# Positions added during mixing, two expert loads moved forward, and buffers cleared by another engine in a trunk layer on one Trainium2 core

## Chip, cores and metric

One core of one Trainium2 chip runs the whole program as one launch. The metric is the device time in microseconds. All arithmetic is 32-bit float, with a few integer steps in the routing. The names: PE is TensorE, PEld its weight load, DVE VectorE, ACT ScalarE, POOL GpSimd, SP SyncE, which issues most transfers.

## What is computed

One layer of a trunk over 128 prompt tokens and 512 sample tokens of width 1024. A bidirectional RWKV-7 scan and a gated convolution are mixed, projected by `w_out` and added to the tokens; then a mixture of experts (32 experts in 4 groups, two of one group for each token) is added, and a final norm follows. Cut to what matters here:

```python
xs = x_sample + grid_pos_embed(rows)          # positions: a constant table
def trunk_layer(x, cond, s0, p):
    sh1, sc1, g1, sh2, sc2, g2 = adaln_mod(cond, p['ada_w'], p['ada_b'])
    h = rms_norm(x, p['norm1_g']) * (1 + sc1) + sh1
    z = h @ p['w_in']
    y_rwkv, s_new = rwkv7_bidir(...)
    y_conv = conformer_conv(...)
    x = x + g1 * (concatenate([y_rwkv, y_conv]) @ p['w_out'])
    h = rms_norm(x, p['norm2_g']) * (1 + sc2) + sh2
    x = x + g2 * hier_moe(h, p)
    return x, s_new
```

## The kernel before

Each engine runs one program; they meet in semaphores. The stages follow one another in all of them: front (norm and modulation), mix, out, route, experts, overflow, end.

**Mix.** The columns of `w_in` are multiplied tile by tile ("z" steps, L582, a quarter tile each) while the scan's preparation and its steps are laced in between, in an order written out by hand for PE, ACT, DVE and SP (`ORDER`, L655). There are five scan units; four hold the sample tokens, the fifth the prompt. Each unit's preparation runs on DVE and ACT (L1050 to L1111: scans, scaled keys and their products) and feeds gram matrices on PE (L1275). GpSimd has nothing to do in this stage after it has stored the last block of modulation rows at L536. The convolution is done tile by tile in two buffers, `uin` and `cacc`; each of four tiles is stored to DRAM (L801) and loaded back at L858 when the scan's room is free. The last convolution tile is stored at about 205 us; the memory of `uin` and `cacc` (from `conv_at`) is unused from then on. The experts' weight buffers, six of 3 MB (`ebuf`, L1404), lie on top of the scan's memory; the first two lie over the buffers of the units with odd numbers.

**Out.** `sp_out` (L1467) loads the tokens again as residual rows `x2` (five tiles of 128 rows and 512 KB), the modulation rows `g1b`, `gain2`, `sh2b`, and stores the final states. PE multiplies tile after tile (order `WTILES`: 1, 2, 3, 4, 0) by `w_out`, two halves of 512 columns each (L1640, sixteen matmuls for a half), turns each finished tile (L1609) and computes its 36 router logits (L1624). `act_out` loads the positions of the next tile into one buffer `sq_pos` (L1892). On DVE, `residual` adds the positions (L1765) and then the gated projection in two halves (L1770, L1771); `taken` copies half of a turned tile out of a bank (L1757); `top_two` (L1793 to L1811) picks group and experts; `expert_input` (L1778 to L1784) forms the experts' input row, which ACT stores to DRAM with the residual rows (L1909, L1910). DVE's first wait in this loop is for all five residual tiles and both `g1b` rows (L1750).

**Route.** DVE and PE count rows per expert, sort the experts and write a table of slots (L1984 to L2062). The list of experts is ready at L2005 (`s_ids`), the table at L2060 (`s_tab`). GpSimd clears the row buffers `xe` with one memset when `w_out` is done (L2098), since tiles of a pair or of four can have empty rows.

**Experts.** 16 tiles of rows run in a fixed order: each needs one, two or four experts. GpSimd gathers each tile's rows (L2108) and scatters its results (L2114). PE turns the rows (L2332), multiplies by gate and up weights (L2348), turns the hidden rows (L2357) and multiplies by the down weights (L2369). SP loads 32 experts, 1 MB each for gate, up and down (L1510). The experts of the first three loads are fixed; they are loaded behind `sp_out`. The later ones need `s_ids`. The fourth load is issued at once, the fifth and sixth wait for the first gather (`s_gat[0]`), and from the seventh on each waits until the tile that used its buffer has been multiplied.

## Time and profile before

| | us |
|---|---|
| median of 3 runs (lowest, highest) | 1085.02 (1084.62, 1087.08) |
| the profiled execution | 1084.78 |
| its span | 1083.1 |
| PE busy | 899.6 (83%) |
| DVE busy | 590.1 (54%) |
| ACT busy | 287.6 (27%) |
| POOL busy | 61.7 (6%) |

The page also cuts the span in 40 slices of 27 us. These are its rows of busy tenths (9 is 90% or more), of TensorE's granted clock in tenths of full speed, and of the transfers:

```profile
PE   3899988999988697878967997796698797997786
DVE  5239999765267767677761455567524132331325
PEclk9899988999988677585685899797599898998998
DMA  9952642210100202001018168411599999999874
GB/s 355 329 217 59 238 187 100 82 59 10 21 2 11 22 1 31 3 11 21 2 21 195 51 210 346 178 59 78 189 421 420 420 420 406 406 422 382 337 272 197
```

Slice 24 begins at 623 us. The mix ends about there, out and route run to 776 us, the experts to about 1055 us. A busy engine is not by itself the bound of a stretch; the chain of waits and the idle time ahead of an instruction, with what ended it, tell that.

### The profile page before, as it was taken

The numbers are of one execution on the slowest core, as the hardware profiler recorded it, in microseconds if no ns is written. First come the engines' busy times: TensorE is split into PE (matmuls) and PEld (weight loads), VectorE is DVE, ScalarE is ACT, GpSimd is POOL, SyncE is SP. The second block draws the span as 40 slices with busy tenths as digits, with TensorE's granted clock in tenths as the row PEclk, the third lists the DMA queues.
The fourth block names the chain that finished last, engine by engine and source line by source line (L and its number), as shares of the span: only waits on it lengthen the run. The fifth ranks groups of instructions, "written<-read, shape, count | busy, mean of one in ns | idle before, by whom it ended". The sixth has DMA issues, their size and how long they took to land.

```text
span 1083.1 us, 17415 instructions
## 1 busy us (share of the span) xinstructions
PE 899.6 (83%) x6856; PEld 543.4 (50%) x6856; DVE 590.1 (54%) x1197; ACT 287.6 (27%) x506; POOL 61.7 (6%) x63
## 2 busy tenths in 40 slices
PE   3899988999988697878967997796698797997786
PEld 2466444567665675757747653444333242442232
DVE  5239999765267767677761455567524132331325
ACT  4230010331755646377212351011110000000002
POOL 0100000000000000000000000001111110111023
PEclk9899988999988677585685899797599898998998
DMA  9952642210100202001018168411599999999874
GB/s 355 329 217 59 238 187 100 82 59 10 21 2 11 22 1 31 3 11 21 2 21 195 51 210 346 178 59 78 189 421 420 420 420 406 406 422 382 337 272 197
DMA packets 74292, 194.74 MB, mean 180 GB/s; under 512 B 41888, under 2 KB 44354, under 8 KB 60004
## 3 DMA queue, kind: packets, MB, share of 16 engines
q1 hardware_dynamic: 65988, 175.30, 43.9%
q0 software_dynamic: 5728, 10.79, 2.7%
q10 hardware_dynamic: 2495, 7.54, 1.8%
q8 instruction: 55, 0.90, 0.3%
q14 instruction: 26, 0.21, 0.1%
HBM read 180.68 MB, written 21.31 MB: 187 GB/s over the span
## 4 chain that ended last, share of the span: by engine, by line
PE 44%; DVE 16%; DMA 13%; ACT 7%; issue 4%; SPq 1%; ACTq 0%; DVEq 0%
PE bank L2348 9%; PE bank L582 8%; DMA arena<-in_expert_w_up 8%; PE bank L2369 3%; DMA arena<-table_positions 3%; PE bank L1640 3%; DVE arena L1022 2%; PE bank L1262 2%; PE bank L1275 2%; PE bank L1332 2%; PE bank L1361 1%; ACT arena L898 1%; PE bank L1335 1%; DMA arena<-winv 1%; DVE arena L1119 1%
## 5 line engine op out<-in xcount | busy, mean ns | idle before, releaser
L582 PE MATMUL bank<-arena 128*128 128x320 f32 x704 | 207.3, 448 | 2.6 <-ACT arena L410 2.6
L582 PEld LDWEIGHTS bank<-arena 128*128 128x128 f32 x704 | 133.5, 194 | 77.0 <-issue 27.4
L2348 PE MATMUL bank<-arena 128*64 128x512 f32 (+2 forms) x496 | 124.0, 673 | 24.5 <-DMA arena<-in_expert_w_up 23.6
L1022 DVE SCALAR_TENSOR_TENSOR arena<-arena 128x655 f32<-128x655 f32 x116 | 104.7, 902 | 4.4
L2348 PEld LDWEIGHTS bank<-arena 128*64 128x64 f32 (+2 forms) x496 | 44.5, 152 | 102.3 <-issue 101.0
L2451 DVE TENSOR_TENSOR arena<-arena,bank 128x256 f32<-128x256 f32 x16 | 6.7, 422 | 130.9 <-ACT arena L2410 130.9
L1640 PE MATMUL bank<-arena 128*128 128x512 f32 x160 | 74.5, 622 | 0.0
L2369 PE MATMUL bank<-arena 128*64 128x512 f32 (+2 forms) x248 | 58.8, 599 | 9.4 <-DVE arena L2454 9.4
L2410 ACT ACTIVATE arena<-bank 128x256 f32<-128x256 f32 x16 | 6.2, 385 | 201.9 <-PE bank L2348 201.8
L1640 PEld LDWEIGHTS bank<-arena 128*128 128x128 f32 x160 | 31.0, 198 | 37.3 <-issue 37.1
L1361 PE MATMUL bank<-arena 64*64 64x64 f32 x320 | 33.1, 263 | 13.0 <-DVE arena L1189 13.0
L1361 PEld LDWEIGHTS bank<-arena 64*64 64x64 f32 x320 | 27.8, 170 | 25.8 <-DVE arena L1189 19.2
L2369 PEld LDWEIGHTS bank<-arena 128*64 128x64 f32 (+2 forms) x248 | 19.2, 138 | 38.1 <-issue 25.7
L1119 DVE TENSOR_TENSOR arena<-bank,arena 128x512 f32<-128x512 f32 x40 | 27.7, 693 | 14.9 <-PE bank L1275 13.9
L2098 POOL MEMSET arena<- 128x4096 f32 x1 | 3.5, 3512 | 541.1 <-PE bank L1640 541.1
L981 ACT ACTIVATE arena<-bank 64x128 f32<-64x128 f32 (+1 forms) x68 | 19.9, 292 | 51.9 <-PE bank L1361 45.6
L1050 DVE SCALAR_TENSOR_TENSOR arena<-arena 128x512 f32<-128x512 f32 (+1 forms) x48 | 26.6, 553 | 12.8 <-ACT arena L898 11.2
L1189 DVE TENSOR_TENSOR arena<-bank,arena 64x128 f32<-64x128 f32 (+1 forms) x68 | 20.9, 307 | 21.4 <-PE bank L1352 18.7
L1275 PE MATMUL bank<-arena 64*128 64x128 f32 x320 | 25.9, 305 | 7.2 <-issue 1.7
L898 ACT ACTIVATE arena<-arena 128x512 f32<-128x512 f32 (+1 forms) x48 | 27.0, 563 | 15.1 <-DVE arena L1134 6.3
L1262 PE MATMUL bank<-arena 128*128 128x512 f32 x40 | 28.2, 804 | 2.3 <-ACT arena L917 2.3
L1297 PE MATMUL bank<-arena 64*64 64x64 f32 x320 | 28.4, 255 | 1.7 <-ACT arena L908 1.7
(360 smaller groups left out, 1351.2 us busy)
## 6 DMA issues: line engine op xcount, KB each, us to landing
arena<-in_expert_w_gate SPq DMA_DIRECT2D x33, 1024.0 KB, 18.7
arena<-in_expert_w_up SPq DMA_DIRECT2D x33, 1024.0 KB, 24.3
arena<-in_expert_w_down SPq DMA_DIRECT2D x33, 1024.0 KB, 23.5
arena<-in_ada_w SPq DMA_DIRECT2D x12, 2048.0 KB, 10.4
arena<-in_w_in SPq DMA_DIRECT2D x22, 512.0 KB, 4.4
arena<-expert_rows SPq DMA_DIRECT2D x10, 512.0 KB, 7.3
arena<-in_x_sample SPq DMA_DIRECT2D x8, 512.0 KB, 6.8
arena<-in_w_out SPq DMA_DIRECT2D x1, 4096.0 KB, 15.3
```

What stands on the lines that cost most here:

```text
L582: mm = nc.tensor.matmul(psum[4 + 2 * (n % 2) + half][:, 0:HALF], wring[:, n % NWIN, k], hT[:, k, half * HALF:(half + 1) * HALF], start=(pa ...
L898: ins_ = nc.scalar.activation(X[:, s[4]:s[4] + s[3]], previous(zrkv[:, 4 * m + s[1], :], s), ACT.Copy, scale=par[:, c:c + 1])
L1022: chain(nc.vector.scalar_tensor_tensor(acc, src, w, acc, ALU.mult, ALU.add))
L1050: ins_ = nc.vector.scalar_tensor_tensor(x, current(zrkv[:, 4 * m + s[1], :], s), oneminus[:, c:c + 1], x, ALU.mult, ALU.add)
L1119: chain.announce(nc.vector.tensor_tensor(GM[b][:, GC * (q % 2) + 4 * (q // 2):GC * (q % 2) + 4 * (q // 2) + 4, :], psum[BANK[f"g{q}"]][:, ...
L1262: nc.tensor.matmul(psum[BANK[f"{name}{h}"]][:, :], headones, T0[:, 512 * h:512 * h + 512], start=True, stop=True).then_inc(s_summed, 1)
L1275: mm = nc.tensor.matmul(psum[BANK[f"g{q + h}"]][:, n * P:(n + 1) * P], BK[r, gc_, :], AR[b][r, gc_, :], start=True, stop=True)
L1297: mm = nc.tensor.matmul(psum[BANK[f"m{q}"]][0:64, n * C:(n + 1) * C], GM[b][64:128, GC * h + g0 + n, 0:C], SAV[b][64:128, g0 + n, C * h:C ...
L1361: mm = nc.tensor.matmul(psum[6 + h][0:64, k * C:(k + 1) * C], GM[b][0:64, GC * h + gc_, 0:C], XS[0:64, at:at + C], start=True, stop=True)
L1640: mm = nc.tensor.matmul(psum[2 * ((q + 1) % 2) + n][:, :], lhs, wout[:, c, n * 512:(n + 1) * 512], start=(c == 0), stop=(c == 7))
L2348: mm = nc.tensor.matmul(psum[2 + n % 2][r, :], xeT[:, n % 2, c, r], gu[:, :, c, :], start=(c == 0), stop=(c == KD - 1))
L2369: mm = nc.tensor.matmul(psum[5 + h][r, :], hidT[:, n % 2, c, r], wd[:, c, h * 512:(h + 1) * 512], start=(c == 0), stop=(c == 1))
```

## The change

Four things are done.

1. `pool_mix`, new: when the convolution's tiles are stored, GpSimd loads each of the four sample tiles and its positions into the free memory at `conv_at`, adds them, and stores the sum to `placed` in DRAM. `sp_out` takes the residual rows of tiles 1 to 4 from there. The adds in `residual`, the buffer `sq_pos`, its loads on ACT and the semaphore `s_pos2` go. The load of tile 4 counts in `s_modb`, so that DVE's first wait is for six loads.
2. `sp_out` begins with the loads of the first two fixed experts, behind waits for `placed` and for the last step of the fourth unit. The third follows behind `sp_out`. After the lists two experts are loaded ahead of the wait for the first gather, not one.
3. The buffers `xe` are cleared by four ACT copies with scale 0 (`act_route`), which now runs inside `act_out`, ahead of the last tile's stores. `pool_experts` waits for it.
4. For the last tile, the row's scale is computed on its own (`row_scale`), then `top_two`, then `expert_input`.

```diff
+        placed = dram("tokens_with_positions", [TS, D])
+        tok_in, pos_in = view(conv_at, D), view(conv_at + D, D)
+        def pool_mix(chain):
+            pool = nc.gpsimd
+            for stored in s_cst:
+                pool.wait_ge(stored, 32)
+            for i in range(1, TILES):
+                if i > 1:
+                    pool.wait_ge(s_placest, 16 * (i - 1))
+                pool.dma_start(tok_in, tok_src(i)).then_inc(s_sl, 16)
+                pool.dma_start(pos_in, pos[(i - 1) * P:i * P, :]).then_inc(s_sl, 16)
+                pool.wait_ge(s_sl, 16 * 8 + 32 * i)
+                chain(nc.gpsimd.tensor_tensor(tok_in, tok_in, pos_in, ALU.add))
+                pool.dma_start(placed[(i - 1) * P:i * P, :], tok_in).then_inc(s_placest, 16)
 ...
         def sp_out():
             sp = nc.sync
+            sp.wait_ge(s_placest, 16 * (TILES - 1))
+            sp.wait_ge(s_Y, step_at(NU - 2, steps(NU - 2) - 1) + 1)
+            for n in range(len(FIXED_EXPERTS) - 1):
+                experts_load(n)
             sp.wait_ge(s_gvar, 5)
-            for i in (1, 2, 3, 0):
-                sp.dma_start(x2[:, i], tok_src(i)).then_inc(s_x2in, 16)
+            for i in (1, 2, 3):
+                sp.dma_start(x2[:, i], placed[(i - 1) * P:i * P, :]).then_inc(s_x2in, 16)
+            sp.dma_start(x2[:, 0], tok_src(0)).then_inc(s_x2in, 16)
 ...
-            sp.dma_start(x2[:, 4], tok_src(4)).then_inc(s_x2in, 16)
+            sp.dma_start(x2[:, 4], placed[3 * P:4 * P, :]).then_inc(s_modb, 16)
 ...
-            dve.wait_ge(s_x2in, 16 * (TILES + 2))
+            dve.wait_ge(s_x2in, 16 * (TILES + 1))
 ...
             def residual(q, n):
-                if i and n == 0:
-                    dve.wait_ge(s_pos2, 16 * i)
-                    chain(nc.vector.tensor_tensor(x2[:, i], x2[:, i], sq_pos, ALU.add))
 ...
-            dve.wait_ge(s_modb, 16 * 6)
+            dve.wait_ge(s_modb, 16 * 7)
 ...
             residual(q, 1)
             taken(q)
+            row_scale(q)
+            top_two(q)
             expert_input(q)
-            top_two(q)
 ...
             for q, i in enumerate(WTILES):
-                if i:
-                    if q:
-                        act.wait_ge(s_x2, 2 * (q - 1) + 1)
-                    act.dma_start(sq_pos, pos[(i - 1) * P:i * P, :]).then_inc(s_pos2, 16)
 ...
+                if q == TILES - 1:
+                    act_route(chain)
                 act.wait_ge(s_h2, q + 1)
 ...
         def act_route(chain):
             act = nc.scalar
+            act.wait_ge(s_wo, 2 * TILES)
+            for n in range(NG):
+                ins_ = nc.scalar.activation(xe[:, n], ones[:, 0:1].broadcast_to([P, D]), ACT.Copy, scale=0.0)
+                if n < NG - 1:
+                    chain(ins_)
+            chain.announce(ins_, s_ge, 1)
             act.wait_ge(s_mx, TILES)
 ...
-        def pool_route(chain):
-            pool = nc.gpsimd
-            pool.wait_ge(s_wo, 2 * TILES)
-            chain(nc.gpsimd.memset(xe, 0.0))
 ...
         def pool_experts(chain):
             pool = nc.gpsimd
+            pool.wait_ge(s_ge, 1)
             pool.wait_ge(s_tab, 1)
 ...
             sp_out()
-            sp.wait_ge(s_pos2, 16)
-            for n in range(len(FIXED_EXPERTS)):
-                experts_load(n)
+            experts_load(len(FIXED_EXPERTS) - 1)
             sp.wait_ge(s_ids, 1)
             sp.wait_ge(s_h2st, 32 * TILES)
             sp.dma_start(gain_step[0:2], modrows[:, 5 * D:6 * D]).then_inc(s_fg, 16)
-            experts_load(len(FIXED_EXPERTS))
+            for n in range(len(FIXED_EXPERTS), NB - 1):
+                experts_load(n)
             sp.wait_ge(s_gat[0], 16)
-            for n in range(len(FIXED_EXPERTS) + 1, NB):
-                experts_load(n)
+            experts_load(NB - 1)
```

## Rows read from the trace of the kernel before

**Rows 1.** Timeline of PE, 640 to 760: start, us, line, shapes, [idle before, releaser].

```profile
648.26 14.00 PE L1640 MATMUL bank<-arena 128*128 128x512 f32 x32
...
669.53 1.04 PE L1609 MATMUL bank<-arena 128*128 128x128 f32 x8
683.84 3.63 PE L1624 MATMUL bank<-arena 128*128 128x36 f32 x16 [13.28 <-DVE arena L1832]
...
703.26 1.04 PE L1609 MATMUL bank<-arena 128*128 128x128 f32 x8
704.54 1.98 PE L1624 MATMUL bank<-arena 128*128 128x36 f32 x16 [0.25 <-ACT arena L1885]
...
720.17 1.04 PE L1609 MATMUL bank<-arena 128*128 128x128 f32 x8
...
733.38 1.03 PE L1609 MATMUL bank<-arena 128*128 128x128 f32 x8
```

**Rows 2.** The chain of waits from 640 on: start, us, what.

```profile
665.55 15.20 DMA arena<-table_positions
```

**Rows 3.** Busy us by engine in two stretches; last the clock, DMA share, GB/s.

```profile
205.00:255.00 50.00, 48.29 (x224) 32.56 (x223) 28.01 (x36) 18.27 (x28) 0.00 (x0) 1.00 0.16 50
...
780.30:843.00 62.70, 52.27 (x214) 21.32 (x213) 19.64 (x31) 5.83 (x11) 9.91 (x10) 0.94 1.01 410
```

**Rows 4.** Timeline of PE in the expert stage.

```profile
779.60 1.97 PE L2332 MATMUL bank<-arena 128*128 128x128 f32 x8 [0.60 <-DMA arena<-tokens_for_experts,arena]
...
843.09 9.81 PE L2348 MATMUL bank<-arena 128*32 128x512 f32 x64 [5.47 <-DMA arena<-in_expert_w_up]
```

**Rows 5.** Timeline of DVE, 649 to 1061.

```profile
649.63 0.09 DVE L1813 MEMSET arena<- 128x32 f32 x1 [9.14 <-DMA arena<-in_x_sample]
...
743.11 3.57 DVE L1807 TENSOR_SCALAR arena<-arena 128x32 f32<-128x32 f32 x1
...
748.09 0.69 DVE L1771 TENSOR_TENSOR arena<-arena 128x512 f32<-128x512 f32 x1
...
752.78 1.28 DVE L1784 SCALAR_TENSOR_TENSOR arena<-arena 128x1024 f32<-128x1024 f32 x1
754.10 0.25 DVE L1793 SCALAR_TENSOR_TENSOR arena<-bank,arena 128x36 f32<-128x36 f32 x1
...
758.48 0.21 DVE L1984 TENSOR_SCALAR arena<-arena 2x128 f32<-2x128 f32 x1
...
1060.90 0.69 DVE L2511 TENSOR_TENSOR arena<-arena,bank 128x512 f32<-128x512 f32 x1 [3.92 <-issue]
```

**Rows 6.** Timeline of GpSimd (POOL).

```profile
743.13 3.51 POOL L2098 MEMSET arena<- 128x4096 f32 x1 [541.11 <-PE bank L1640]
776.07 1.09 POOL L2108 DMA_INDIRECT arena<-tokens_for_experts,arena  x1 [29.42 <-DVE arena L2060]
...
1060.99 2.37 POOL L2189 TENSOR_TENSOR arena<-arena 128x1024 f32<-128x1024 f32 x1 [0.22 <-DMA arena<-expert_rows]
```

**Rows 7.** Timeline of ACT: a 128x1024 activation.

```profile
748.87 1.06 ACT L1904 ACTIVATE arena<-arena 128x1024 f32<-128x1024 f32 x1 [4.68 <-DVE arena L1771]
```

**Rows 8.** Timeline of SP's queue: issue time, us of issuing.

```profile
204.58 0.33 SPq L801 DMA_DIRECT2D conv_out<-arena  x1
...
780.31 0.34 SPq L1510 DMA_DIRECT2D arena<-in_expert_w_gate  x1
```

**Rows 9.** DMA issues: count, KB each, median us from issue to landing.

```profile
residual_rows<-arena ACTq DMA_DIRECT2D x5, 512.0 KB, 3.9
...
arena<-tokens_for_experts,arena POOLq DMA_INDIRECT x18, 10.9
```

**Rows 10.** Timelines of DVE and PE in the mixing.

```profile
229.36 1.13 DVE L1082 TENSOR_SCALAR arena<-arena 128x512 f32<-128x512 f32 x2
...
240.41 1.54 DVE L1111 SCALAR_TENSOR_TENSOR arena<-arena 128x512 f32<-128x512 f32 x2
...
240.48 1.16 PE L1275 MATMUL bank<-arena 64*128 64x128 f32 x16 [1.71 <-issue]
```

More of the change, by code:

```diff
@@ L784, in build @@
         s_cst = [sem(f"conv_tile_stored{b}") for b in range(2)]
+        s_placest = sem("placed_tokens_stored")
         def sp_mix():
@@ L1427, in build @@
         g1b, gain2 = regs.take(2, D), regs.take(2, D)
-        h2, sq_pos = regs.take(D), regs.take(D)
+        h2 = regs.take(D)
         rwg, lgc = regs.take(2, KD * 36), regs.take(2, 36)
@@ L1450, in build @@
         s_cn, s_mixc = sem("conv_normed"), sem("conv_mixed")
[L1451 removed]
+        s_x2in = sem("residual_landed")
         s_wo, s_x2, s_h2, s_h2st = (sem(n) for n in (
@@ L1771, in residual, with row_scale @@
                 chain.announce(nc.vector.tensor_tensor(x2[:, i, o], x2[:, i, o], xtmp[:, o], ALU.add), s_x2, 2 * q + n + 1)
+            def row_scale(q):
+                i = WTILES[q]
+                dve.wait_ge(s_xstat, TILES + q + 1)
+                chain.announce(nc.vector.tensor_scalar(small[:, i:i + 1], small[:, i:i + 1], 1.0 / D, RMS_EPS,
+                                                     ALU.mult, ALU.add), s_var, TILES + q + 1)
+                dve.wait_ge(s_std, TILES + q + 1)
+                chain(nc.vector.reciprocal(small[:, 16 + i:17 + i], small[:, 8 + i:9 + i]))
             def expert_input(q):
@@ L1778, in expert_input @@
                 chain(nc.vector.tensor_tensor(h2, x2[:, i], gain2[:, int(i > 0)], ALU.mult))
-                dve.wait_ge(s_xstat, TILES + q + 1)
-                chain.announce(nc.vector.tensor_scalar(small[:, i:i + 1], small[:, i:i + 1], 1.0 / D, RMS_EPS,
-                                                     ALU.mult, ALU.add), s_var, TILES + q + 1)
-                dve.wait_ge(s_std, TILES + q + 1)
-                chain(nc.vector.reciprocal(small[:, 16 + i:17 + i], small[:, 8 + i:9 + i]))
+                if q < TILES - 1:
+                    row_scale(q)
                 chain.announce(nc.vector.scalar_tensor_tensor(h2, h2, small[:, 16 + i:17 + i], sh2b[:, int(i > 0)],
@@ L1844, in dve_out @@
             taken(q)
+            row_scale(q)
+            top_two(q)
             expert_input(q)
-            top_two(q)
         def act_out(chain):
@@ L2065, in act_route @@
             act = nc.scalar
+            act.wait_ge(s_wo, 2 * TILES)
[4 more added lines that the diff above has]
+            chain.announce(ins_, s_ge, 1)
             act.wait_ge(s_mx, TILES)
-            chain.announce(nc.scalar.activation(gexp, gexp, ACT.Exp), s_ge, 1)
-            chain.announce(nc.scalar.activation(t3, t3, ACT.Exp), s_ge, 2)
+            chain.announce(nc.scalar.activation(gexp, gexp, ACT.Exp), s_ge, 2)
+            chain.announce(nc.scalar.activation(t3, t3, ACT.Exp), s_ge, 3)
         def pe_route():
@@ L2561, in _ @@
             act_out(chain)
-            act_route(chain)
             act_table()
@@ L2582, in _ @@
             pool_front()
-            pool_route(chain)
+            pool_mix(chain)
             pool_experts(chain)
```

8 lines of the change are left out of this document (4 added, 4 removed).

## Prediction

> **What bounds the kernel now.** I read the 40 slices of the page first (PE at 9 tenths almost everywhere, DMA at 9 only from slice 29 on), then the chain of waits after the mixing, then the timelines of PE, DVE, GpSimd and SyncE's queue over the stretches that the chain names. Times are positions in the profiled span. Three stretches matter. From 205 to 285 us PE is full, and the change puts new GpSimd work beside it. From 640 to 776 us (output projection and routing) PE stops: it stands for 13.28 us ahead of the logits of the first tile [rows 1], because DVE waits for a 512 KB tile of positions, which took 15.20 us to land [rows 2] while the nine loads of three fixed experts filled the queues. From 780 us on the expert weights stream at 410 GB/s with the DMA share at 1.01 [rows 3]; PE waits for them at the four-expert tiles (5.47 us at 843.09 [rows 4]). So an earlier start helps in full only if the stream starts earlier too.
>
> **Position waits (a gain).** In the changed kernel the residual rows come with positions in them, so four adds on DVE and four loads on ScalarE's queue go. DVE's first wait now lasts until 649.63 and ends with an in_x_sample tile [rows 5], the one for tile 4, which the change counts in another semaphore; the six loads that are left in that wait should be in by about 645. Even a start at 649.6 would be free: DVE's next residual needs the second half of tile 1, which is the first half of PE's 14.00 us block from 648.26 and ends at 655.3 [rows 1]. DVE then has its residuals, gains, first expert input and prompt mixing done by about 668.7 (I follow the same instructions as now without the positions). PE's turn of the first tile stays at 669.53 [rows 1], and its logits follow at once. From there PE bounds the loop. An undisturbed round, turn to turn, is 720.17 - 703.26 = 16.91 us [rows 1] (this one had a late position tile too, but it held up DVE, not PE). DVE has about 11 us of work in a round: top-two 758.48 - 754.10 = 4.4 [rows 5], residuals and copy some 3.6, expert input 3.3. So the second turn comes at 669.53 + 16.91 = 686.4 in place of 703.26: **16.8 us**. The third keeps this. Between third and fourth turn lies one half less, 16.91 - 7.0 = 9.9 us, where the trace has 733.38 - 720.17 = 13.2 [rows 1] (DVE's copy late by a position tile, and a slower matmul block): **3.3 us** more.
>
> **Row buffers cleared by ScalarE (a gain).** GpSimd's memset ran from 743.13 for 3.51 us [rows 6], and DVE's TENSOR_SCALAR at 743.11 took as long, 3.57 us, where a TENSOR_SCALAR of 2x128 takes 0.21 [rows 5]; it stood in the top-two that holds back the last residual. Without it **3.3 us** go. The four ScalarE copies cost about 1.06 us each, as the 128x1024 Square does [rows 7]: 4.3 us, between the last root and the exponentials. DVE's top-two (4.4 us) covers them, so nothing is on the path; without that cover it would be at most 4.3. Together the last residual, now done at 748.09 + 0.69 = 748.8 [rows 5], comes 23.4 us sooner, at 725.4.
>
> **New order behind it (a loss).** Top-two no longer waits for the last expert input, but for the logits: about 1 us behind the residual for the turn, then sixteen matmuls, 3.63 us with PE cold (683.84) and 1.98 warm (704.54 [rows 1]), so 3.0 to 4.6 us behind it. Then come 4.4 us of top-two and 2.6 us of expert input (two 128x1024 instructions, 1.28 the longer [rows 5]). Route starts 10.0 to 11.6 us behind the residual; now it is 758.48 - 748.8 = 9.7. Cost 0.3 to 1.9; PE idles less than before, so near the low end: **-0.7**. Left: 22.7 us at the table of slots.
>
> **Two fixed experts earlier, one more between lists and gather.** The two early loads (6.3 MB, 15.4 us at 410 GB/s) are issued at about 597 us, behind the convolution's loads on the same queue, into a stretch that is empty until 632. Nothing else is queued behind them but the waits on SyncE, which come later. The third still goes out near 656. After the lists, SyncE now issues two experts ahead of its wait for the first gather, not one: now one near 763, then nothing until 780.31 [rows 8]. In the changed kernel the lists are ready near 740, but the last store of rows (it is behind the moved expert input, and such a store takes 3.9 us to land [rows 9]) makes it about 742. Two experts, 6.3 MB, then run until 742 + 1.7 + 15.4 = 759. The gather is issued at 776.07 - 22.7 = 753.4 [rows 6], and would land 3.5 us later on an empty fabric; beside the loads its median is 10.9 us [rows 9], so it crawls until 759 and lands at about 760. PE starts to turn the rows at 779.60 [rows 4]; then at 760: 19.6 us sooner. Cost of the contention **-3.1** (0 if it shares evenly, 7.4 if it takes the median).
> What a page would make of this: the Trainium skill, "DMA: Bandwidth & Descriptors", section "Queues, rings and completion order", says that each engine goes round between the queues it has work for, packet by packet. Read as even shares that would let the gather land near 758.5 and give 1.5 us back (1061.5); the median of 10.9 us under load speaks against it, so the sum goes by the row.
>
> **The stream.** Counted from the first gather, the stream has one expert less to bring: 3.15 MB, 7.7 us. Against it stands new idle time, since six buffers are then full until the first gate-up matmuls end (9.4 us after they start): 2 to 3 us. PE's wait of 5.47 us at the first four-expert tile [rows 4] thus shrinks to a rest below 1: **+4.6** (bounds 0 and 5.5). From there on the stream is full, and everything, tail included, keeps its distances.
>
> **GpSimd in the mixing (a loss).** Twelve DMAs and four 128x1024 adds of 2.37 us [rows 6] begin once the last convolution tile, stored at 204.58 [rows 8], has landed. A turn of that loop is two loads (some 4 us), the add, and a store (some 3 us) that the next turn waits for, about 11 us: adds near 212, 223, 234 and 245, over by 251, far ahead of 632. DVE works without a pause from 229.36 or earlier to 240.41 + 1.54 = 241.95, and PE already waits 1.71 us for this at 240.48 [rows 10]. The add near 234 falls into it. The trace has two cases of GpSimd beside DVE: the memset that stopped a TENSOR_SCALAR with both ends in the arena, and an add at 1060.99 beside which L2511, with one operand in a bank, took 0.69, as L1771 does [rows 5, 6]. DVE's instructions here have all operands in the arena, and two of them are TENSOR_SCALARs of that form [rows 10]. I take the blocked case for one add: **-2.35**; bounds 0 and 4.7 (two adds). The others meet DVE where it has slack, or reads a bank. PE is full from there to 285, so nothing gives it back.
> The page "SBUF — State Buffer" of the Trainium skill (its practical consequences of port sharing) says that a DVE instruction with two SBUF inputs and a GpSimd instruction that reads SBUF shut each other out, and that a DVE one with one SBUF input outside the 2-port modes is free. No row here shows the two-input case. If only the TENSOR_SCALAR form blocked, the sum would lose this term most likely (1060.6).
>
> **Sum.** 16.8 + 3.3 + 3.3 - 0.7 - 3.1 + 4.6 - 2.35 = 21.85 us. The profiled execution took 1084.78 us (span 1083.1), the median of the runs is 1085.02, 0.2 above. 1085.0 - 21.9 gives **1063.1**.
>
> **Rivals.**
> - No add holds up DVE's chain: 1060.7. For it, L2511; against it, L1807. 0.22.
> - The gather takes its median of 10.9 us, so PE starts 4.3 us later than I have it, and the four-expert tile waits as now (4.6): 1067.4 to 1072. For it, the median of 18 gathers; against it, that only the second half of two loads runs beside it. 0.18.
> - The change does less than it says: the position wait was a wait for the shared queues, and the one fixed expert still issued near 656 (7.7 us) holds up the stores of the first tile, for which DVE's second expert input waits. Then 1070.8. Against it, that stores of DVE's first input leave at 665, when that load is through. 0.07.
> - Slower than before: DVE gets nothing done while GpSimd runs its 44 us loop. DVE is busy for 28.0 us between 205 and 255 [rows 3]; put behind the loop, they cost 28.0 - 2.35 us more than in the sum, 1088.8. It decides from 24 us of blocked DVE on. The adds last 9.5 us in all, so 0.02.
> - My forecast, with the terms within their near bounds (1061.3 to 1066): 0.51.
>
> **How the numbers follow.** Likeliest 1063.1. To hold 8 in 10 the range takes in the first rival with a fully saved quad wait and even sharing (1058) and the second up to 1069. What a measurement can tell from no change is about 0.2%, 2.2 us. Faster needs under 1082.9, which all but the last rival give: 0.975; same 0.01; slower 0.015.
>
> **What the profile would show.** PE's wait at the first logits gone and its second turn near 689 (686.4 plus the 2.35 of the mixing); no 3.5 us DVE instruction near the last top-two; DVE's last residual near 728; first gather landed near 762; less than 1 us of wait at the first four-expert tile; an add of GpSimd inside DVE's chain near 234, with one DVE instruction 2 us too long, and PE's wait at 240 grown to 4. I am wrong if the gather lands over 5 us behind the end of the loads, if PE waits for DVE inside the rounds, or if z quarters start late by more than one add.

## The result

The changed kernel takes **1070.66 us** (median of 4 runs, 1068.16 to 1072.89) where the kernel before takes 1085.74 beside it (4 runs). The ratio is 0.9858, 95% interval 0.9838 to 0.9878: 1.4% faster. Three runs that lie far above all others of their kernels (1456.11 us in e1, 1108.04 in e2, and 3813.41 of the kernel before in the group of e5, e6, e7 and a2) are left out of the medians and ratios.

The direction of the forecast holds. Its time, 1063.1, is 7.6 us too low, and the range of 1058 to 1069 does not hold the result. Later groups gave the same changed kernel ratios of 0.9862 (0.9824 to 0.99) and 0.9875 (0.9849 to 0.9902).

The profiled execution of after took 1072.89 us (span 1071.2, against 1083.1 before). From the page:

| | before | after |
|---|---|---|
| span, profiled | 1083.1 us | 1071.2 us |
| PE busy | 899.6 us (83%) | 905.6 us (85%) |
| GpSimd (POOL) busy | 61.7 us (6%) | 74.0 us (7%) |
| GpSimd's DMA queue | 10.79 MB | 17.09 MB |

The page's slices of after, GpSimd and the granted clock in tenths (one slice is 26.8 us):

```profile
POOL 0100000131000000000000000000101111011023
PEclk9899988998987759585586699997599899999899
```

Slices 8 to 10 (counted from 1, 187 to 268 us) hold what is new: GpSimd works in them, and in the tenth the clock reads 8 where it is 9 in before.

First what the forecast said of the output stage. PE's timeline in after, the turns of the five token tiles (the rows that answer to [rows 1]):

```profile
679.20 1.04 PE L1632 MATMUL bank<-arena 128*128 128x128 f32 x8
680.58 1.95 PE L1647 MATMUL bank<-arena 128*128 128x36 f32 x16 [0.34 <-ACT arena L1912]
...
696.17 1.04 PE L1632 MATMUL bank<-arena 128*128 128x128 f32 x8
...
713.09 1.04 PE L1632 MATMUL bank<-arena 128*128 128x128 f32 x8
...
723.20 1.04 PE L1632 MATMUL bank<-arena 128*128 128x128 f32 x8
...
735.33 0.66 PE L1632 MATMUL bank<-arena 128*128 128x128 f32 x4 [2.01 <-DVE arena L1791]
```

The logits wait 0.34 us where they waited 13.28, the second turn comes 16.97 us behind the first (forecast 16.91), the fourth 10.11 behind the third (9.9), and the second half of the last one 12.1 behind that. Only the first turn stands in the wrong place: 679.20, 9.7 us later than in before [rows 1]. All of that was lost ahead of the output stage, in the mixing: 8.4 us of it up to 260 us, 2.2 from there to 649 us, where the traces scatter by more than that (below), less 0.9 us by which after was ahead at 199 us. VectorE and PE in before, where the first addition will fall and at one of the instructions that the third will meet:

```profile
212.08 1.54 DVE L1050 SCALAR_TENSOR_TENSOR arena<-arena 128x512 f32<-128x512 f32 x2 [1.75 <-ACT arena L898]
215.25 1.12 PE L1262 MATMUL bank<-arena 128*128 128x512 f32 x2
...
232.31 1.23 DVE L1087 TENSOR_TENSOR arena<-arena 128x1024 f32<-128x1024 f32 x1
```

VectorE, GpSimd and PE in after (L1068 is the L1050 of before, L1105 its L1087, L1280 its L1262):

```profile
211.25 3.51 DVE L1068 SCALAR_TENSOR_TENSOR arena<-arena 128x512 f32<-128x512 f32 x2 [1.75 <-ACT arena L916]
211.83 2.38 POOL L875 TENSOR_TENSOR arena<-arena 128x1024 f32<-128x1024 f32 x1 [4.10 <-DMA arena<-table_positions]
...
216.39 1.16 PE L1280 MATMUL bank<-arena 128*128 128x512 f32 x1 [1.93 <-ACT arena L935]
...
235.07 2.35 POOL L875 TENSOR_TENSOR arena<-arena 128x1024 f32<-128x1024 f32 x1 [4.48 <-DMA arena<-table_positions]
235.16 3.35 DVE L1105 TENSOR_TENSOR arena<-arena 128x1024 f32<-128x1024 f32 x1
...
245.44 2.08 PE L1293 MATMUL bank<-arena 64*128 64x128 f32 x16 [3.84 <-issue]
...
247.59 0.69 DVE L1137 TENSOR_TENSOR arena<-bank,arena 128x512 f32<-128x512 f32 x1
247.66 2.35 POOL L875 TENSOR_TENSOR arena<-arena 128x1024 f32<-128x1024 f32 x1 [5.65 <-DMA arena<-table_positions]
```

Two additions, not one, have a VectorE instruction beside them that is about 2 us too long (3.51 for 1.54, 3.35 for 1.23), and PE waits behind each: 1.93 us at 216, where before has no wait, and 3.84 where [rows 10] has 1.71. Behind the second wait sixteen matmuls of L1293 take 2.08 us where [rows 10] has 1.16. The fourth addition runs beside L1137, which reads a bank, and costs it nothing. Busy time by engine, clock, DMA share and GB/s in two stretches, first of before, then of after:

```profile
205.00:235.00 30.00, 30.00 (x109) 19.71 (x108) 14.77 (x19) 17.05 (x24) 0.00 (x0) 1.00 0.22 64
235.00:260.00 25.00, 23.29 (x136) 16.32 (x136) 13.24 (x18) 2.41 (x6) 0.00 (x0) 1.00 0.13 32
```

```profile
205.00:235.00 30.00, 28.07 (x96) 17.94 (x95) 14.01 (x16) 14.62 (x21) 9.16 (x10) 0.94 0.53 185
235.00:260.00 25.00, 21.16 (x116) 14.80 (x115) 16.71 (x19) 2.06 (x4) 6.92 (x6) 0.86 0.33 119
```

The granted clock, 1.00 in before, is 0.94 and 0.86. Two short stretches right behind the waits show where it was down, at the lower of its two levels (1.2 and 2.4 GHz):

```profile
216.40:219.50 3.10, 3.10 (x5) 1.68 (x6) 0.69 (x1) 0.00 (x0) 1.07 (x2) 0.51 0.42 110
245.40:247.40 2.00, 1.96 (x16) 1.81 (x16) 1.93 (x3) 0.00 (x0) 0.00 (x0) 0.50 0.73 299
```

The clearing of the row buffers and the expert stage of after (rows that answer to [rows 7], [rows 6] and [rows 4]):

```profile
737.29 4.32 ACT L2093 ACTIVATE arena<-arena 128x1024 f32<-128x1024 f32 x4
742.43 1.28 ACT L2098 ACT_TABLE_LOAD   x1 [0.82 <-DVE arena L1837]
```

```profile
763.12 1.07 POOL L2134 DMA_INDIRECT arena<-tokens_for_experts,arena  x1 [512.23 <-DVE arena L2085]
```

```profile
769.93 1.97 PE L2359 MATMUL bank<-arena 128*128 128x128 f32 x8 [1.31 <-DMA arena<-tokens_for_experts,arena]
...
827.72 7.07 PE L2375 MATMUL bank<-arena 128*32 128x512 f32 x64 [0.75 <-DMA arena<-in_expert_w_up]
845.43 10.01 PE L2375 MATMUL bank<-arena 128*64 128x512 f32 x32 [4.83 <-DMA arena<-in_expert_w_up]
```

The wait of the first four-expert tile is gone (0.75 for 5.47 [rows 4]), but the next tile now waits 4.83. In before it waits 1.77:

```profile
860.49 7.09 PE L2348 MATMUL bank<-arena 128*64 128x512 f32 x32 [1.77 <-DMA arena<-in_expert_w_up]
```

**One execution is not the kernel.** Seventeen traces were taken in all, four of them of the kernel before. The time between fixed VectorE instructions splits each into stages. The marks, in after's lines, are the L1042 that starts at 198.65 in after (ahead of the first unit; in all traces it starts between 197.6 and 200.7), the last row of L1137 in that unit (259.50), L1743 (649.02, start of the output stage), L1780 (724.33), L2009 (744.97, start of the routing), L2448 (772.04, first expert tile) and the L2478 at 835.40 (first four-expert tile) and at 1003.25 (last static tile), and L2310 (1023.39, first overflow tile). Stage lengths in us, worked out from VectorE's timelines:

```
                      to 259 to 649 to 724 to 745 to 772 to 835 to 1003 to 1023
before                 52.48 387.28  95.16  23.97  23.22  71.81  165.03  16.74
b2_before_again        52.53 389.75  93.88  23.82  25.69  68.25  164.23  20.14
b3_before_again        52.30 389.35  94.07  23.83  25.69  68.38  163.77  20.13
b4_before_again        52.36 387.31  95.13  23.98  25.70  66.41  165.20  18.48
e3_loop_alone          58.15 385.01  93.47  23.84  25.69  68.98  163.97  16.75
after                  60.85 389.52  75.31  20.64  27.07  63.36  167.85  20.14
a2_after_again         58.30 386.29  75.30  20.78  27.23  64.56  166.11  16.76
a3_after_again         56.86 391.66  75.30  21.49  27.47  63.70  167.72  19.77
e7_double_add          60.71 388.45  75.30  21.59  27.03  63.83  167.73  19.68
e4_one_ahead           58.19 385.34  75.31  20.65  25.69  66.29  167.25  16.74
e5_memset_back         58.15 387.53  75.30  25.77  27.09  64.68  166.22  19.62
e6_fixed_late          58.27 388.70  75.30  20.65  27.13  63.47  167.82  19.71
e1_no_add              52.51 389.61  75.29  21.50  27.12  64.32  166.96  20.16
e11_memset_not_add     52.74 389.72  75.30  21.49  27.11  64.19  168.25  16.75
e10_copy_not_add       54.16 387.32  75.30  20.74  27.00  66.18  165.60  18.47
e2_gated               52.41 387.18  75.29  22.35  27.58  63.99  166.29  16.75
e8_gated_again         52.47 389.56  75.30  21.49  27.18  64.69  166.67  20.17
```

Behind the last mark all take 47.7 to 48.3. Read down a column: where all kernels with a part of the change differ from all without, it is the part; where one kernel differs from itself, it is the execution. "To 649" (385.0 to 391.7 over all) and "to 1023" are of the second kind.

### The profile page after: what moved, and what is told of

The parts are those of the page before. It is cut to its first block, busy times and chain, and to the rows that moved or that the text cites. A ratio compares the mean times of both kernels' runs of the same rounds, so it can differ in the third digit from the quotient of the medians.

```text
span 1071.2 us, 17424 instructions
## 1 busy us (share of the span) xinstructions
PE 905.6 (85%) x6856; PEld 547.9 (51%) x6856; DVE 585.8 (55%) x1193; ACT 291.9 (27%) x510; POOL 74.0 (7%) x78
## 3 DMA queue, kind: packets, MB, share of 16 engines
q0 software_dynamic: 7456, 17.09, 4.3%
## 4 chain that ended last, share of the span: by engine, by line
PE 49%; DVE 15%; DMA 10%; ACT 6%; issue 3%; SPq 1%; DVEq 0%; ACTq 0%; POOLq 0%
PE bank L2375 9%; PE bank L582 8%; DMA arena<-in_expert_w_up 7%; PE bank L1663 6%; PE bank L2396 4%; DVE arena L1040 2%; PE bank L1293 2%; PE bank L1353 2%; PE bank L1350 2%; PE bank L1280 1%; ACT arena L916 1%; PE bank L1379 1%; DMA arena<-winv 1%; PE bank L1305 1%; DVE arena L1137 1%
## 5 line engine op out<-in xcount | busy, mean ns | idle before, releaser
L582 PE MATMUL bank<-arena 128*128 128x320 f32 x704 | 212.1, 456 | 2.4 <-ACT arena L410 2.4
L2478 DVE TENSOR_TENSOR arena<-arena,bank 128x256 f32<-128x256 f32 x16 | 6.8, 422 | 124.9 <-ACT arena L2437 124.9
L1663 PE MATMUL bank<-arena 128*128 128x512 f32 x160 | 70.6, 595 | 0.0
L2134 POOL DMA_INDIRECT arena<-tokens_for_experts,arena x17 | 17.2, 1015 | 521.9 <-DVE arena L2085 512.2
L1379 PE MATMUL bank<-arena 64*64 64x64 f32 x320 | 32.3, 258 | 14.1 <-DVE arena L1207 14.0
L1137 DVE TENSOR_TENSOR arena<-bank,arena 128x512 f32<-128x512 f32 x40 | 27.7, 693 | 18.0 <-PE bank L1293 17.0
L1293 PE MATMUL bank<-arena 64*128 64x128 f32 x320 | 27.3, 317 | 9.7 <-issue 3.8
L1068 DVE SCALAR_TENSOR_TENSOR arena<-arena 128x512 f32<-128x512 f32 (+1 forms) x48 | 28.5, 594 | 12.0 <-ACT arena L916 10.5
L999 ACT ACTIVATE arena<-bank 64x128 f32<-64x128 f32 (+1 forms) x68 | 19.9, 292 | 52.0 <-PE bank L1379 50.5
L1280 PE MATMUL bank<-arena 128*128 128x512 f32 x40 | 28.7, 818 | 3.7 <-ACT arena L935 3.7
L1293 PEld LDWEIGHTS bank<-arena 64*128 64x128 f32 x320 | 23.4, 219 | 16.2 <-issue 15.6
L1305 PE MATMUL bank<-arena 128*128 128x128 f32 x160 | 28.2, 317 | 4.1 <-DVE arena L1085 1.7
```

Of the source, the lines that this page charges most:

```text
L582: mm = nc.tensor.matmul(psum[4 + 2 * (n % 2) + half][:, 0:HALF], wring[:, n % NWIN, k], hT[:, k, half * HALF:(half + 1) * HALF], start=(pa ...
L1068: ins_ = nc.vector.scalar_tensor_tensor(x, current(zrkv[:, 4 * m + s[1], :], s), oneminus[:, c:c + 1], x, ALU.mult, ALU.add)
L1137: chain.announce(nc.vector.tensor_tensor(GM[b][:, GC * (q % 2) + 4 * (q // 2):GC * (q % 2) + 4 * (q // 2) + 4, :], psum[BANK[f"g{q}"]][:, ...
L1280: nc.tensor.matmul(psum[BANK[f"{name}{h}"]][:, :], headones, T0[:, 512 * h:512 * h + 512], start=True, stop=True).then_inc(s_summed, 1)
L1293: mm = nc.tensor.matmul(psum[BANK[f"g{q + h}"]][:, n * P:(n + 1) * P], BK[r, gc_, :], AR[b][r, gc_, :], start=True, stop=True)
L1305: mm = nc.tensor.transpose(psum[BANK[f"{name}{q}"]][:, n * P:(n + 1) * P], src, ident)
```

## The experiments

**e1: no additions.**

```
-                chain(nc.gpsimd.tensor_tensor(tok_in, tok_in, pos_in, ALU.add))
```

> The kernel after without the four GpSimd additions of L875; its loads and stores stay, so the rows of the last four token tiles lack their positions. Theory (in the mixing stage VectorE's instructions with two inputs in SBUF wait behind a GpSimd addition, two of the four additions lie on PE's path, and the granted clock falls after each): out's first matmul L1663 comes about 9 us earlier relative to the start than in the kernel after, and the time is 1061 to 1063 us (1070.7 less 8 to 10), a ratio to the kernel before near 0.978. L1068 at about 210 us falls from 3.51 to 1.54 for two, L1105 at about 235 us from 3.35 to 1.23. Rival (the descriptors, the loads and stores of GpSimd, or a clock that drifts with the chip): the time stays at 1069 to 1072 us and the stalls stay.

Measured: a median of 1065.2 us (5 runs), a ratio of 0.9799 (0.977 to 0.9829). The first stage takes 52.51 us, as in before, though GpSimd's twelve transfers are all there. It is the additions and not the traffic. L1068 is back at 1.54 us and the two-input instructions near 235 us at 1.23. The 8 to 10 us expected, and with them 1061 to 1063 us, are missed: the gain is about 6 in the time (from the 1071.1 of all runs of the kernel after, below). The trace of after, from which they were worked out, is the dearest of its kind in the first column.

**e2: the same additions, in VectorE's calm.**

```
                 pool.wait_ge(s_sl, 16 * 8 + 32 * i)
+                if i == 1:
+                    pool.wait_ge(s_rk, 1)
+                elif i == 3:
+                    pool.wait_ge(s_inv, 1)
+                elif i == 4:
+                    pool.wait_ge(s_cs, 2)
                 chain(nc.gpsimd.tensor_tensor(tok_in, tok_in, pos_in, ALU.add))
```

> The kernel after with the same four additions, each held back to a stretch in which VectorE has no instruction with two inputs in SBUF: the first behind the bonus product of the first unit (about 242 us), the second follows it by some 11 us, the third behind the inverse of the first unit (about 271 us), the fourth behind the decay sums of the second unit (about 296 us). The output is whole. Theory (lock, then clock): no stall of VectorE, out's first matmul about 9 us earlier than in the kernel after, 1061 to 1064 us. Rival (any GpSimd addition costs, wherever it lies, through its traffic or its power): 1068 to 1072 us. If the stall alone were gone but the clock fell anyway: about 1066 us.

Measured: a median of 1066.1 us (5 runs), a ratio of 0.9816 (0.9789 to 0.9842). The first stage takes 52.41 us with all four additions in the kernel. GpSimd's and VectorE's rows at the first one:

```profile
242.50 2.35 POOL L881 TENSOR_TENSOR arena<-arena 128x1024 f32<-128x1024 f32 x1 [33.30 <-DVE arena L1135]
```

```profile
242.91 1.42 DVE L1143 TENSOR_TENSOR arena<-bank,arena 128x512 f32<-128x512 f32 x2
```

L1143 has one input in a bank and takes its 1.42 us. The third and fourth addition lie behind the first stage, at 272 and 296 us, in a column that is as in before. So the same four additions cost nothing in these places; the rival "any addition costs" falls. The time is 2 us above the 1061 to 1064 expected and equals the 1066 of the rival "the clock falls anyway", but the trace rules that one out: the granted clock is 1.00 from 205 to 300 us.

**e3: the loop alone, on the kernel before.**

```
             sp.wait_ge(s_pos2, 16)
+            sp.wait_ge(s_placest, 16 * (TILES - 1))
             for n in range(len(FIXED_EXPERTS)):
...
+            pool_mix(chain)
```

> The kernel before with GpSimd's loop of loads, additions and stores alone; nobody reads what it stores, and the residual adds its positions as before. Its price by itself. By the trace of the kernel after: two additions on the path and the clock after them, 8 to 10 us slower than the kernel before, 1093 to 1095 us. By the forecast's step (one addition on the path, 2.35 us): 1087.4 us. By the rival that the lost time of the mixing stage is a matter of the execution and not of the loop: within 1 us of 1085.

Measured: a median of 1089.9 us (12 runs), a ratio of 1.0039 (1.0021 to 1.0056), 4.2 us above the kernel before by the ratio: between the two theories (1093 to 1095, and 1087.4). Its first stage is 58.15, 5.7 longer than the 52.4 of the kernel before, and no other column is longer than in before. Two VectorE instructions are too long again, 3.71 us near 212 (for 1.54) and this one:

```profile
235.85 2.48 POOL L874 TENSOR_TENSOR arena<-arena 128x1024 f32<-128x1024 f32 x1 [4.28 <-DMA arena<-table_positions]
236.15 3.26 DVE L1112 SCALAR_TENSOR_TENSOR arena<-arena 128x1024 f32<-128x1024 f32 x1
```

**e7: every addition twice.**

```
                 chain(nc.gpsimd.tensor_tensor(tok_in, tok_in, pos_in, ALU.add))
+                chain(nc.gpsimd.tensor_tensor(pos_in, tok_in, pos_in, ALU.add))
```

> The kernel after with every GpSimd addition of the mixing stage followed by a second one of the same size, whose result nobody reads. Theory (VectorE's two-input instructions wait behind GpSimd's additions, and the clock falls with the stalls): each blocked instruction lasts up to 4.7 us and not 3.4, and more of them are hit, since GpSimd adds for 19 us of some 56 and not for 9.4 of 45: 4 to 10 us slower than the kernel after, 1075 to 1081 us. Rival (the additions themselves cost nothing, the loss of the mixing stage comes from elsewhere): within 1.5 us of 1070.7.

Measured: a median of 1070.5 us (6 runs), a ratio of 0.985 (0.9819 to 0.9881). By the time the expectation of 4 to 10 us more is a miss. The trace says what happened in its place. The doubled turn lasts 14 to 16 us and not 11, so the additions meet other instructions:

```profile
229.15 2.88 POOL L875 TENSOR_TENSOR arena<-arena 128x1024 f32<-128x1024 f32 x1 [4.99 <-DMA arena<-table_positions]
229.86 4.95 DVE L1101 TENSOR_SCALAR arena<-arena 128x512 f32<-128x512 f32 x2
...
243.47 3.26 DVE L1126 TENSOR_TENSOR arena<-arena 128x1024 f32<-128x1024 f32 x1
...
245.73 3.21 POOL L876 TENSOR_TENSOR arena<-arena 128x1024 f32<-128x1024 f32 x1
...
246.83 2.08 PE L1294 MATMUL bank<-arena 64*128 64x128 f32 x16 [7.58 <-issue]
```

More instructions are held up, as expected, but none for two additions: the two instructions of L1101 take 2.46 us each (for 0.57), one beside each addition (the second addition runs from 232.11 for 2.42 us). The first addition meets the scan L1077 (3.26 us for 1.23) and no longer L1069 (the L1068 of after), and PE has no wait at 216. Its second wait has grown to 7.58 us for the 1.71 of before, and behind it the matmuls lose 2.4 us. Together that is the first stage of 60.71, 2.5 us longer than the 58.2 of most single-addition traces and no longer than that of after. The times do not tell these 2.5 us.

**e10 and e11: a copy, and a memset, in the additions' place.**

```
-                chain(nc.gpsimd.tensor_tensor(tok_in, tok_in, pos_in, ALU.add))
+                chain(nc.gpsimd.tensor_copy(pos_in, tok_in))      e10
+                chain(nc.gpsimd.memset(pos_in, 0.0))              e11
```

> The kernel after with a GpSimd copy (one input in SBUF) where the addition (two inputs) stood; the rows of the last four tiles lack their positions. A look at what on GpSimd's side holds VectorE. If any GpSimd instruction that reads SBUF does, L1068 or its neighbours still last longer than 1.54 us by about the copy's own length, and so do those at 235 us; if only a two-input instruction of GpSimd does, they show 1.54 and 1.23 us and the mixing stage loses nothing.

> The kernel after with a GpSimd memset (no input, it only writes) of one row buffer where the addition stood; the rows of the last four tiles lack their positions. If VectorE waits for any GpSimd instruction that touches SBUF, L1068 and L1105 or their neighbours grow by about the memset's length; if it waits only for one that reads, they stay at 1.54 and 1.23 us. The last residual of the kernel before took 3.57 us beside a memset, so by that row a stall is expected.

One run each (1063.15 and 1063.56 us); the rows of the last four tiles go without their positions here, as in e1. Timelines of GpSimd and VectorE at the third turn, e10 first:

```profile
231.89 1.04 POOL L875 COPY arena<-arena 128x1024 f32<-128x1024 f32 x1 [4.27 <-DMA arena<-table_positions]
232.01 1.99 DVE L1105 TENSOR_TENSOR arena<-arena 128x1024 f32<-128x1024 f32 x1
```

```profile
231.21 0.95 POOL L875 MEMSET arena<- 128x1024 f32 x1 [4.24 <-DMA arena<-table_positions]
231.32 1.23 DVE L1105 TENSOR_TENSOR arena<-arena 128x1024 f32<-128x1024 f32 x1
```

Beside the copy L1105 lasts 0.76 us longer (and L1068, near 212, 2.20 us for 1.54); beside the memset it takes its 1.23, and L1068 its 1.54. The first stages are 54.16 and 52.74 us. So VectorE's instruction with two inputs in SBUF waits for a GpSimd instruction that reads SBUF, for what is left of it, and not for one that only writes. That is what the Trainium skill says in "SBUF — State Buffer", section "Who interferes with whom", and the rows agree on both sides.

**a2: the kernel after once more.**

> The kernel after, unchanged, once more, on the same chip as the other kernels of this group: 1068 to 1073 us by its four executions so far. Its trace tells what belongs to one execution and what to the kernel: theory has a loss of 6 to 10 us in the mixing stage in every execution (the stalls of L1068 or its neighbours and of L1105 or its neighbours are there in each), while the 3.4 us that the stretch behind 1000 us lost to the granted clock is a matter of the execution and may be gone.

Measured: a median of 1068.9 us (6 runs, 1063.10 to 1074.03). Its first stage is 58.30, its "to 1023" 16.76 for 20.14 in the first trace. The loss in the mixing comes back, though with 5.9 us just under the 6 to 10 expected; that in the last tiles does not.

**e5: the memset back on GpSimd.** The four ScalarE copies go, and before GpSimd's wait for the table stands again

```
+            pool.wait_ge(s_wo, 2 * TILES)
+            chain(nc.gpsimd.memset(xe, 0.0))
```

> The kernel after with the row buffers cleared by GpSimd again (the 3.5 us memset of before, behind the last product of the output stage) and not by ScalarE. The forecast's step: the last residual of VectorE waits 3.3 us for the memset, everything behind it is 3.3 us later: 1074 us (1070.7 plus 3.3), and the row of the last residual shows about 3.5 us for what takes 0.4 to 1.2 us in the kernel after. Rival (a slack behind it takes it up, as the routing waits for something else): the same 1070.7.

Measured: a median of 1073.5 us (6 runs), a ratio of 0.9896 (0.9859 to 0.9933), 2.5 above the 1071.1 that the three groups of the kernel after give together (16 runs). VectorE and GpSimd in e5:

```profile
729.53 3.56 DVE L1833 TENSOR_SCALAR arena<-arena 128x32 f32<-128x32 f32 x1
729.55 3.51 POOL L2141 MEMSET arena<- 128x4096 f32 x1 [477.41 <-PE bank L1663]
```

The 3.3 us stall is back to the tenth. The stage grows from 20.6 to 22.4 (all others with the change) to 25.77, that is by 3.4 to 5.1. The stall is the forecast's. And here a memset does hold up VectorE: a TENSOR_SCALAR with one input in SBUF. The Trainium skill names that form too, in "SBUF — State Buffer", section "Who interferes with whom" (an instruction of VectorE's 2-port modes and any of GpSimd's), and lets a two-input one pass beside a memset, as e11 shows.

**e6: the two fixed experts late again.** Their loads move from the head of the output stage's SyncE list to its end, in front of the third.

> The kernel after with the two early loads of fixed experts put back behind the output stage's loads, as in the kernel before; the order of the routed experts' loads stays new. By the forecast the early loads carry nothing by themselves, since the stretch of 640 to 750 us moves only some 180 GB/s: within 1 us of the kernel after, 1070 to 1072 us. Rival: the transfers of the output stage's rows and of the fourth unit compete with the 6.3 MB (at 400 GB/s some 16 us of all queues), so that the residual's rows or the first routed expert come late: 2 to 8 us slower, with a wait for DMA at the first residual or at the first expert tile.

Measured: a median of 1069.5 us (6 runs), a ratio of 0.9857 (0.9828 to 0.9885), and every stage from 649 us on as in after within 0.5 us (75.30, 20.65, 27.13, 63.47, 167.82, 19.71). The early loads carry nothing by themselves; the rival falls.

**e4: one routed expert ahead of the first gather.**

```
-            for n in range(len(FIXED_EXPERTS), NB - 1):
-                experts_load(n)
+            experts_load(len(FIXED_EXPERTS))
             sp.wait_ge(s_gat[0], 16)
-            experts_load(NB - 1)
+            for n in range(len(FIXED_EXPERTS) + 1, NB):
+                experts_load(n)
```

> The kernel after with one routed expert's load ahead of the wait for the first gather in SP's queue, as before, and not two. The two fixed experts stay early. By the forecast's steps: the first gather lands sooner by some 3.3 us (less traffic beside it), and the wait of the four-expert tile L2348/L2371 for its weights comes back by 4.6 to 5.1 us: 1.3 to 1.8 us slower than the kernel after, near 1072.3 us. If the next wait for weights (4.83 us at 845 us) swallows what that step gains, the time is the same or 1 to 2 us less than the kernel after.

Measured: a median of 1070.6 us (6 runs), a ratio of 0.9855 (0.9817 to 0.9892). The gather's stage is 25.69 for 27.07 (1.4 sooner, not 3.3), the next 66.29 for 63.36 (2.9 later, not 4.6 to 5.1): up to the first four-expert tile (745 to 835 us) the second expert ahead is worth 1.6 us in the trace, up to 1003 us 0.7 against the mean of the traces with it, which is within their scatter, and it is worth nothing that the times can tell. The other theory of that line, 1 to 2 us less than after, isn't shown either.

**b2, b3, b4: the kernel before, three more traces.** No edit.

> The kernel before, unchanged, for its trace alone. If the 3.0 to 3.4 us that 7 of 12 traces with the change lose between the last static tile and the overflow tile (L2396 5.35 us for 3.65, L2234 8.80 for 7.10) belong to the change, every trace of the kernel before shows 3.65 and 7.10; if they are a matter of the execution, some of three show the long ones.

> The kernel before a second time. As for b2_before_again; the distance from the last static tile's residual (1018.54) to the first of the overflow (1035.28) is 16.7 us in the trace of before so far, and 19.7 to 20.2 in the slow traces of the kernel after.

> The kernel before a third time. As for b2_before_again. It also tells how far the stretch from 300 to 640 us scatters in the kernel before; with the change it differed by up to 6 us from trace to trace.

PE's last static tile and first overflow tile in b2:

```profile
1018.19 5.35 PE L2369 MATMUL bank<-arena 128*64 128x512 f32 x16 [0.58 <-DVE arena L2454]
...
1027.50 8.80 PE L2207 MATMUL bank<-arena 128*128 128x512 f32 x16 [2.87 <-DVE arena L2281]
```

These are the long ones. The stage is 20.14 and 20.13 us in two of the three, 18.48 in the third, 16.74 in the trace on which the forecast rested. So the 3.4 us are a matter of the execution, with and without the change. The same three show something else: the gather's stage is 25.7, not 23.22, and the first four-expert tile waits about 3 us (2.42 to 3.10), not 5.47. That trace was unusual twice. The first shows in PE's row of the eight matmuls of one row ahead of the first expert tile, in before and then in b2:

```profile
774.36 4.64 PE L2379 MATMUL bank<-arena 2*128 2x512 f32 x8
```

```profile
774.92 7.19 PE L2379 MATMUL bank<-arena 2*128 2x512 f32 x8
```

The granted clock is 0.78 over the first of these rows and 0.50 over the second.

The stretch from 259 to 649 scatters by 2.5 us between the four traces of before and by 6.3 between the twelve with the change; nothing here says whether the change adds to it.

**a3 and e8: after and the gated version, side by side.**

> The kernel after, unchanged, beside e8_gated_again: 1069.8 us, by the median of its ten executions so far (1063.1 to 1074.0). In its trace the loss up to 260 us is 5.7 to 8.4 us; the last 70 us take either what they take in the kernel before or 3.4 us more.

> The kernel after with its four additions held back to VectorE's calm stretches (the version of e2_gated, unchanged), once more beside the kernel after on one chip. Theory: nothing is lost up to 260 us in any execution (the first kernel-after executions lost 5.7 to 8.4 us there), so it is 3 to 7 us faster than the kernel after in the same group, 1062 to 1068 us in the median; the spread of some 7 us between executions stays, since it comes from the granted clock behind 300 us. Rival (the advantage of e2_gated was a matter of the execution): no more than 1.5 us faster.

Measured: after 1073.4 us (6 runs), ratio 0.9875 (0.9849 to 0.9902); gated 1065.6 us (6 runs), ratio 0.9803 (0.9779 to 0.9827). The intervals are apart. The 7.8 us between the medians are a little over the 3 to 7 expected, and after is 3.6 above the 1069.8 expected. First stages: 56.86 and 52.47. The loss of 4.4 us in a3 is below the 5.7 to 8.4 expected, and its trace says why: the first addition came too late to hold L1068 (1.55 us) and held the scan behind it, L1076 (3.27 us for 1.23), and PE had no wait there; only the second wait (3.68) was left. All runs taken together give 1071.1 (16) and 1066.1 (11), 5.0 us, near the 6.0 that the first stages show in the mean. **The gated version beats both kernels**: up to 260 us the positions cost nothing when GpSimd adds where VectorE reads a bank or waits.

## Why the forecast was half right

- **Position waits (16.8 and 3.3): right.** The turns stand at the distances forecast, in every trace with the change: that stage is 75.30 us, 19.9 shorter than in the trace of before, and 19.0 shorter than in the mean of the five traces that add the positions in the output stage (before four times, and e3). Forecast: 20.1.
- **Memset (3.3) and new order (-0.7): right in their sum.** Forecast together 2.6; 3.3 in the two profiles, 2.7 in the means. Only the memset was also taken back by itself (e5); no run shows the new order alone. The four copies of 4.32 us lie beside VectorE's top-two, and the exponentials behind them wait for VectorE, as [rows 7] and [rows 5] had it.
- **Gather (-3.1): right in size for the wrong baseline.** 3.85 between the two profiles, 1.4 against the 25.69 of the four other traces without the change. Without the second expert ahead it is nothing (e4). In those four the eight matmuls of one row (L2379 in before) run 7.19 us at the lower clock and not 4.64, and PE comes to its first tile later without any wait for rows; so part of the gather's time is hidden in most executions.
- **The stream (+4.6): the second step that failed.** The tile gained what was forecast (4.7), but "from there on the stream is full, and everything keeps its distances" is wrong: the very next tile waits 4.83 us where before has 1.77, and 3.1 go back. Against the four other traces without the change, whose means at these two tiles are 3.2 and 3.3 us, the first tile gained 2.3 us in the three traces of the changed kernel and the next gave back 1.6. I take the transfers of all weights together for the bound of both tiles (a DMA share of 1.01 in [rows 3]); no run changes how much is moved, so that is argued and not shown. From 745 to 1003 us the five traces without the change take 258.4 us in the mean, the ten with it (e4 and e5 left out) 258.5: the order of loads bought nothing.
- **GpSimd in the mixing (-2.35): the step that failed first and most.** The loss is 4.4 to 8.4 us in the seven traces with single ungated additions (6.0 in the mean, e3 included), 0 without the additions or with gated ones. What was priced came true: the addition near 234 makes one VectorE instruction about 2 us too long, and PE's wait at 240 grows to 3.84 (forecast 4). Two things were missed. The addition near 212 was taken for harmless ("the others meet DVE where it has slack"), though VectorE's instruction there feeds ScalarE and, through it, PE: some 2 us. And behind the waits PE's clock was down, which no term had. The row that the price leaned on, [rows 6], shows a TENSOR_SCALAR held up by a memset; which forms an addition holds up was open, and the runs show two-input ones (SCALAR_TENSOR_TENSOR, TENSOR_TENSOR, TENSOR_TENSOR_SCAN) as well as a TENSOR_SCALAR (e7). In e6, a trace of the usual kind:

```profile
216.78 1.12 PE L1280 MATMUL bank<-arena 128*128 128x512 f32 x2 [2.09 <-ACT arena L935]
...
244.05 2.08 PE L1293 MATMUL bank<-arena 64*128 64x128 f32 x16 [3.75 <-issue]
246.06 3.06 PE L582 MATMUL bank<-arena 128*128 128x320 f32 x8
```

The waits are 2.09 and 2.04 more than before (3.75 less the 1.71 of [rows 10]), and the slow matmuls 1.6 (2.08 for 1.16, 3.06 for 2.42): 5.7 us, the stage's 5.8. In the trace of after the clock fell behind the first wait too, and the slow matmuls are over 4 us. The term's bounds ended at 4.7, two additions without their clock; the upper end of the range, 1069, came from another rival (the gather) and left no room for it either.
- **The sum against one execution.** Of the 7.6 us, 3.6 are the mixing (6.0 for 2.35), 1.6 the gather and the stream (-0.1 for the 1.5 that 4.6 - 3.1 promised), 1.0 the output stage and routing (21.7 for 22.7). The rest (1.4) is half the base, since the kernel before took 1085.74 here and not 1085.0, and half within the scatter of the other stages. Between the two profiles the miss is larger (21.85 forecast, 11.9 found), since before's has the shortest last stage of all and after's almost the longest: 3.4 us that say nothing of the change.
- **Chances.** "No add holds up DVE's chain" is false as a rival for this kernel, and true of the gated one; its 1060.7 is reached by the best gated run alone (1060.25). Two others gave times near the result (the gather at its median 1067.4 to 1072, the change that does less 1070.8) by mechanisms that the traces do not show: PE had its rows 6.8 us behind the gather's issue (763.12 to 769.93), not 10.9, and the second turn came at its distance. VectorE was never blocked for the whole loop.

## What to carry to other kernels

Before work is put on GpSimd beside VectorE, list VectorE's instructions in that stretch with their operands: a GpSimd instruction that reads SBUF stops those with two inputs in SBUF, an addition and a memset both stop the one-input TENSOR_SCALAR form, and the instructions with an input from a bank were never held up here; then place the work by a semaphore that VectorE announces anyway. Price a stall ahead of a full PE at more than its length, since the clock goes with it (5.7 us for some 4 of stall here). And take two or three traces of the kernel before as the base: the 5.47 us wait that was priced here is 2.4 to 4.2 us in the four others.

## What the hardware showed unexpectedly

- The hold works both ways, and VectorE gets in between two GpSimd additions that follow each other within 0.1 us. In e7 L1126 at 243.47 waits for the first addition (3.26 us for 1.23), and the second, at 245.73, then takes 3.21 us for 2.35, while L1126 runs to its end at 246.73.
- A tenth of a microsecond decides whether PE waits at all. In e6 the first addition starts at 212.25 and the second instruction of L1068 at 212.26; that one then takes 2.89 us for 0.75, and PE waits 2.09. In e7 the same instruction starts at 213.36 and the addition at 213.45; it takes its 0.75, and PE does not wait.
- The same program's traces differ by up to 3.4 us in the last static and first overflow tile alone. In before and b2 these are the same matmuls at another granted clock: 1.00 from 1024 to 1040 us in before, 0.89 in b2, where L2207 takes 8.80 us for 7.10. Nothing that was changed here tells when the clock falls; what decides it stays open.
